# The last tile of each feed-forward by seven half-size products, with its product in SBUF

## The reference

```
def swiglu(h, w_gate, w_up, w_down):
    return (jax.nn.silu(h @ w_gate) * (h @ w_up)) @ w_down
```

## Time and profile before

| | us |
|---|---|
| median of 3 runs | 2514.51 |
| lowest and highest | 2512.61, 2514.9 |
| profiled execution, from the first to the last instruction | 2514.8 |
| mean granted TensorE clock in it, share of full speed | 0.996 |

### The profile page before, as it was taken

How to read it: one execution, slowest core, us unless ns; L and a number is a source line. 1 busy time by engine, 2 the same in 40 slices (tenths; PEclk the granted TensorE clock), 3 DMA queues, 4 the chain that set the end, 5 groups by cost and what they waited for, 6 DMA issues and landing times.

```text
span 2514.8 us, 37950 instructions
## 1 busy us (share of the span) xinstructions
PE 2457.7 (98%) x15202; PEld 2108.7 (84%) x15202; DVE 1726.5 (69%) x2551; ACT 1252.5 (50%) x1799; POOL 1358.7 (54%) x672
## 2 busy tenths in 40 slices
PE   8999999999999999999999999999999999999999
PEld 6899987777789999777887889999877777999987
DVE  5777752888677777586666687776687567777755
ACT  5333343568553433567555553333455685343343
POOL 4677754232457777446544357777444224777754
PEclk9999999999999999999999999999999999999999
DMA  4333333111223333222211133333332113333333
GB/s 142 101 101 101 102 113 113 59 59 55 88 89 105 105 102 104 84 76 84 60 35 35 44 100 101 101 101 109 92 92 84 51 34 101 101 101 101 101 102 124
DMA packets 61790, 223.64 MB, mean 89 GB/s; under 512 B 6704, under 2 KB 6832, under 8 KB 61488
## 3 DMA queue, kind: packets, MB, share of 16 engines
q1 hardware_dynamic: 60928, 218.07, 27.5%
q10 hardware_dynamic: 688, 3.15, 0.3%
HBM read 219.10 MB, written 2.10 MB: 88 GB/s over the span
## 4 chain that ended last, share of the span: by engine, by line
PE 78%; DVE 12%; ACT 6%; issue 3%; DMA 1%; POOL 0%; SPq 0%; DVEq 0%; ACTq 0%
PE ps L661 6%; PE ps L662 6%; PE ps L663 6%; PE ps L586 5%; PE ps L588 5%; PE ps L587 5%; PE ps L578 4%; PE ps L577 4%; PE ps L576 4%; PE ps L1799 2%; PE ps L998 2%; PE ps L1800 2%; PE ps L1801 2%; PE ps L1000 2%; PE ps L999 2%
## 5 line engine op out<-in xcount | busy, mean ns | idle before, releaser
L2970 POOL TENSOR_TENSOR w_lo<-raw,w_hi 128x1024 fp32r<-128x1024 f32 (+1 forms) x405 | 942.3, 2337 | 975.5 <-ACT w_hi L496 974.2
L496 ACT ACTIVATE w_hi<-raw 128x1024 fp32r<-128x1024 f32 (+1 forms) x405 | 397.1, 983 | 661.2 <-PE ps L578 432.2
L2977 POOL TENSOR_TENSOR t_lo<-t_sum,t_hi 128x1024 fp32r<-128x1024 f32 x140 | 336.2, 2423 | 50.2 <-DVE t_sum L773 40.9
L661 PE MATMUL ps<-mid_hi,w_hi 128*128 128x512 f32 x704 | 275.4, 391 | 6.6 <-DVE h L887 3.4
L662 PE MATMUL ps<-mid_lo,w_hi 128*128 128x512 f32 x704 | 274.8, 390 | 0.0
L663 PE MATMUL ps<-mid_hi,w_lo 128*128 128x512 f32 x704 | 273.9, 389 | 0.0
L586 PE MATMUL ps<-sx_hi,t_hi 128*128 128x256 f32 x840 | 238.3, 284 | 5.9 <-DVE ff_up L840 5.9
L588 PE MATMUL ps<-sx_hi,t_lo 128*128 128x256 f32 x840 | 238.0, 283 | 0.0
L587 PE MATMUL ps<-sx_lo,t_hi 128*128 128x256 f32 x840 | 238.0, 283 | 0.0
L887 DVE SCALAR_TENSOR_TENSOR h<-ps,h 128x512 f32<-128x512 f32 x320 | 200.5, 683 | 35.3 <-PE ps L663 25.0
L501 ACT ACTIVATE t_hi<-t_sum 128x1024 fp32r<-128x1024 f32 x140 | 148.0, 1061 | 93.3 <-DVE t_sum L771 51.0
(11 more groups left out here) (455 smaller groups left out, 6456.3 us busy)
## 6 DMA issues: line engine op xcount, KB each, us to landing
raw<-in_units_dram SPq DMA_DIRECT2D x406, 512.0 KB, 3.6
h<-in_x_t_dram SPq DMA_DIRECT2D x4, 512.0 KB, 7.1
toep<-in_rel_table_dram ACTq DMA_DIRECT2D x1, 2048.0 KB, 8.0
out_dram<-h SPq DMA_DIRECT2D x4, 512.0 KB, 5.7
p_f<-in_p_t_dram ACTq DMA_DIRECT2D x2, 512.0 KB, 4.8
const<-in_constants_dram SPq DMA_DIRECT2D x1, 832.0 KB, 7.0
vec<-in_vectors_dram SPq DMA_DIRECT2D x1, 137.5 KB, 2.2
```

The costliest lines, as they stand in the source:

```text
L496: nc.scalar.activation(w_hi[:, n % W_SLOTS, begin:], raw[:, n % RAW_SLOTS, begin:], ACT.Copy).then_inc(s_whi, 1)
L661: nc.tensor.matmul(out, hi, mid_hi[:, mid, :], start=(k == 0), stop=False)
L2970: nc.gpsimd.tensor_tensor(w_lo[:, n % W_SLOTS, begin:], raw[:, n % RAW_SLOTS, begin:], w_hi[:, n % W_SLOTS, begin:].bitcast(F32), ALU.subt ...
L2977: nc.gpsimd.tensor_tensor(t_lo[x % 2][part][:, :, :], t_sum[x % 2][part][:, :, :], t_hi[x % 2][:, 2 * part:2 * part + 2, :].bitcast(F32), ...
```

## The change

`STRASSEN` now reaches to tile 21, so that all tiles from 5 or 3 on have seven products: 74 tiles instead of 70. Whatever is derived from it follows: the weight sums of tile 21 are made in tile 20, `act_round` and the split treat its up unit as half plus sums, SyncE waits for its sums. For tile 21 alone the up half, scaled by rstd, goes to SBUF (`ff_up`) instead of staying in the borrowed bank; the bank is given back right after that multiply, and gate times up, `mid_hi` and `mid_lo` are worked out from SBUF. The other seven-product tiles are as before, but for the place of one wait of VectorE for its own multiply (`s_sv`, now ahead of the wait for Silu).

```diff
-STRASSEN = tuple(range(f, TILES - 1) for f in FIRST)
+STRASSEN = tuple(range(f, TILES) for f in FIRST)
...
-                    product = ps[:, up_bank(g, x), :] if x in picked else ff_up[:, pair, :]
+                    product = ps[:, up_bank(g, x), :] if x in picked and x < TILES - 1 else ff_up[:, pair, :]
...
                 nc.vector.tensor_tensor(c, c, u2, ALU.add).then_inc(s_sv, 1)
                 dve.wait_ge(s_sv, 7 * x + 6)
-                nc.vector.tensor_tensor(up, up, rstd[:, :], ALU.mult).then_inc(s_sv, 1)
+                last = t == TILES - 1
+                home = ff_up[:, pair, :] if last else up
+                nc.vector.tensor_tensor(home, up, rstd[:, :], ALU.mult).then_inc(s_sv, 1)
+                dve.wait_ge(s_sv, 7 * x + 7)
+                if last:
+                    dve.sem_inc(s_free, 1)
                 dve.wait_ge(s_act1, gated + t + 1)
-                dve.wait_ge(s_sv, 7 * x + 7)
-                nc.vector.tensor_tensor(up, up, ff_gate[:, pair, :], ALU.mult).then_inc(s_prod, 1)
+                nc.vector.tensor_tensor(home, home, ff_gate[:, pair, :], ALU.mult).then_inc(s_prod, 1)
                 dve.wait_ge(s_mhi, mids + t + 1)
-                nc.vector.tensor_tensor(mid_lo[:, t % MIDS, :], up, mid_hi[:, t % MIDS, :].bitcast(F32), ALU.subtract).then_inc(s_mlo, 1)
-                dve.wait_ge(s_mlo, mids + t + 1)
-                dve.sem_inc(s_free, 1)
+                nc.vector.tensor_tensor(mid_lo[:, t % MIDS, :], home, mid_hi[:, t % MIDS, :].bitcast(F32), ALU.subtract).then_inc(s_mlo, 1)
+                if not last:
+                    dve.wait_ge(s_mlo, mids + t + 1)
+                    dve.sem_inc(s_free, 1)
```

## The result

The changed kernel took 2545.22 us (median of 4 runs, 2543.43 to 2546.45) beside 2514.66 us: a ratio of 1.0123, 95% interval 1.0111 to 1.0136. It is 30.6 us slower; 27 us were forecast. Its profiled execution took 2546.45 us, of which the span is 2544.6.

A forecast was written before the change was run, and what follows sets the result against it. TensorE, busy 98% of the span, was taken as the bound. To 2514.5 us came 21 us (-0.8 + 5.6 + 0.6 per feed-forward, four times) and 6 us of low clock: 2542 us, range 2529 to 2551.

The forecast's parts named there:

- The products: TensorE at tile 21: 84 short matmuls replace 48 long ones, saving 0.8 us per feed-forward, 3.3 us for four.
- The wait for tile 20's bank and the late Silu: TensorE before tile 21's second product: stands 5.6 us while tile 20's Silu queues behind a rounding awaiting its load.
- The start of the down product: After tile 21, TensorE waits for the last add and multiply: 1.5 us instead of 0.94, 0.6 us more.
- the early give-back: Tile 21's borrowed bank, released early, spares the down product's start another 2.1 us.
- The clock: TensorE after each standstill: one fall to low clock for 3.4 us, losing 1.5 us, 6 us for four.
- no fall of the clock: Rival, chance 0.20: same standstill between tiles 20 and 21, TensorE's clock stays high, 2536 us.
- a short standstill: Rival, chance 0.10: tile 20's Silu doesn't wait for the load; TensorE stands 2.2 to 3.2 us, 2522.5 to 2526.5 us.
- the cover of tile 21's own mid: Down product: three of four row blocks, 8.2 us, hide tile 21's mid, which takes 2 to 3 us.
- The second load of a pair: SyncE's two loads: the second lands within 1 us of the first, hidden by the 5.6 us standstill.

The follow-up runs named there:

- the kernel without pauses: Changed kernel plus early sums, scratch bank of the other group, tile 21's first product copied earlier, down product starting with free banks: 2506.68 us, 0.9972.
- the two kernels that had it: Changed kernel with tile 20's up half in SBUF and its bank given back early: 2542.08 us; the same with tile 21's sums made early: 2528.28 us.

## Why the prediction was right

- **The products** (0.8 us saved each): right, but only the kernel without pauses shows it, 10.07 against 10.91 us.
- **The wait for tile 20's bank and the late Silu** (5.6 us): 5.5, 5.7, 6.2, 5.5 measured. Every link was there: the fourth sum took 0.69 us, the end of the range that was taken; from its end to the rounding it was 3.7, 3.9, 4.4, 3.7 us, where 3.76 was taken from tile 19, and the third pause is the longest because that landing was the latest. Both halves are shown apart: 3.4 us on average go with the Silu's order or with earlier sums, and the other 2.3, all but the 0.4 us of VectorE's order, with another scratch bank.
- **The start of the down product** (0.6 us more; the early give-back worth 2.1): 1.47 - 0.94 = 0.53, and 8.5 us in four when the give-back was undone.
- **The clock** (6 us): the term that was mis-sized. The clock fell at all four pauses, as taken, but not as one fall of 3.4 us behind each: every fall began within the pause, where the first part of it cost nothing, and three of the four lasted 6.8 us. Of the low clock 3.1 to 5.4 us lay behind each pause, and the 72 matmuls lost 1.4 to 2.4 us, 7.1 in all, shown by filling the pause. That the early start and the greater length of the falls nearly make up for one another is luck.
- **Sum:** 22.8 us of pauses + 7.1 of low clock + 2.1 at the down product - 3.3 of products = 28.7 us in the four stretches, where 27 were forecast.
- **Side readings:** the cover of tile 21's own mid is three of the four mids of the down product, not three of four row blocks; it is the same 36 matmuls, and the mid did hide behind them (mid_lo was written 2.1 us after the down product's first matmul). The second load of a pair lands 1.2 to 1.3 us behind the first, not within 1 us, and nothing hung on it.

The rivals "no fall of the clock" (2536) and "a short standstill" (2522.5 to 2526.5) were each made by an experiment: the filled pause gave 2534 us, the Silu ahead of the rounding 2528 us with two falls of the clock in it.

## What to carry to other kernels

A form with less arithmetic that takes its buffers earlier gains only what the wait for those buffers leaves of it. So look at what stands between two such pieces of work everywhere else (here a down product of 5.5 us), and whether it stands there at the new place. Where an engine works ahead in a fixed order, a wait put on work that is not yet needed delays the urgent work behind it: follow the engine's queue, not only the data. And look at the order in which the consumer takes its banks before the producer is made faster: here that order alone took 3.8 us out of the four stretches, and the seven products, once nothing waited, another 3.0.

## What was not expected

- A VectorE multiply of 128 x 512 numbers with both sources in SBUF took 2.6 to 2.8 us beside GpSimd's split of a unit, at seven of the eight tiles 20 of the two kernels that had it, and 0.69 us while GpSimd was idle. In the eighth it began just ahead of the split and took 0.69 us, and the next step, again with both sources in SBUF, took 2.06. The same multiply with one source in PSUM took 0.70 us beside GpSimd's split too. In the changed kernel tile 21's product met an idle GpSimd.
- Behind pauses of the same length, 2.2 to 2.3 us, the clock fell to 0.50 five times in eight (the runs with the Silu first and the sums early); at those of 5.4 us and more (the changed kernel and the one with the late give-back, four times each) it fell every time; where matmuls filled the pause, never.
